# Softmax attention by head pairs on row and column groups of TensorE, in a fused two-layer block

## The chip, the cores and the metric

The kernel runs on one core of a Trainium2 chip. The metric is the device time of one execution in microseconds; the lower the better. All data are fp32.

## What is computed

Two layers over 1024 tokens of 1024 features. The first has four attention branches of four heads of 64 each; the second mixes a convolution, one more attention (E) and two short filters, and ends with a feed-forward part. The change concerns the softmax attention only, of which there are four kinds. Cut to what matters:

```python
# B: banded, window 128, with a sink (called SWA in the kernel)
# A, part 1: compressed keys (32 of them); part 2: selected blocks, here all of them (SEL)
# A, part 3: banded, window 512 (WIN)
s = einsum("qhd,khd->hqk", q, k) * Dh**-0.5 - slope[h] * (q_pos - k_pos)
p = masked_softmax(s, mask, sink)            # rows of queries, over keys
o = einsum("hqk,khd->qhd", p, v)
y_a = g0 * o_cmp + g1 * o_sel + g2 * o_win   # gates per token and head
# E: forgetting attention (FGT), c = cumsum(log_sigmoid(f))
s = q @ k * Dh**-0.5 + c[q] - c[k];  o = softmax(s, causal) @ v
```

SWA, SEL, WIN and FGT have 4 heads and 8 blocks of 128 queries each. A block of queries sees at most 2, 8, 5 and 8 blocks of keys. Everything else in the layers is projections: products of 1024 x 1024 activations with blocks of 128 weight columns.

## The kernel before

Each engine has its own program, written by walking one list of events, `TIMELINE`. The list is made by hand-written rules: the dense work is cut into parts, ("dense", block, part), one part being one 128-deep slice of a block, six matmuls of 512 columns (three products, since an fp32 operand is split into a high and a low fp32r part). The function `spread` lays the steps of an attention stage between the dense parts in proportion to a weight that `weight(ev)` gives each step. Each engine executes its share of each event in this order, so an engine that waits at one event holds back all its later ones, the dense parts too.

One softmax step before is ("soft", u): `unit(u)` is one head `h` and one block `i` of queries, 128 units in all, 32 to each of SWA, SEL, WIN and FGT. The step is a software pipeline over three units:

- PE (`soft` on the tensor engine): the value products of unit u-3 (L865: weights are the transposed probabilities in `ptr`, which is `pbuf[1]`, 128 x 128; 64 value columns stream), the transposes of unit u-2 in groups of four blocks (L843, into `ps6`), then the scores of unit u (L894: 64 rows, since a head is 64 deep; three products of up to 512 key columns, into `ps4`), and masks by bf16 matmuls (L897, L899). The trace counts a fp32 value product as two records, an fp32r product and a transpose as one.
- DVE: adds the bias to the scores (L1893, L1889) into one of three ring buffers `sring`, takes the negated maximum (L1899), makes the factor, 1 over the sum times the gate, in small steps (L1872 to L1879), and scales the output of unit u-3 into `ytok`, tokens on partitions (L1854, L1859).
- ACT: the exponential with its sum (L1318), the copies of the transposes from `ps6` to `ptr` (L1309), the high part of the next query tile (L1384); POOL makes its low part (L1598). Both heads of a pair use one query tile, 128 features.

The softmax output in `ytok` is turned to features on partitions by `ytrans` (L738, eight transposes for each half of a branch) before it is multiplied with the gate `z`. FGT needs the row of c over all keys on every partition; four broadcasts (L1052) make it, one for each head, and ACT copies it to `cb` (L1377). In the second layer, DVE copies the two transposed halves of E out (L2183) in the event "mix".

SWA lies between the parts of merge block D, SEL and WIN between those of merge block C (80 parts each), behind the five steps of the compressed branch (`cmp`, with pauses), and FGT between projections of layer 2, with DVE's convolution taps also in the list.

Of the kernel before, what the change touches and what calls it, by code (L numbers as in the profile page):

```python
# [7 lines left out]
ALU = mybir.AluOpType  # L8
# [89 lines left out]
def weight(ev):  # L98

    if ev[0] == "soft":  # L100
        u, first, n = ev[1:]
        return 1.5 + sum(0.5 * unit(v)[4] for v in (u, u - 2) if first <= v < first + n)
    if ev[0] == "stick" and ev[1] < NSTICK:
        return 1.0 + (HALF - stick_q0(ev[1])) / P
    return 5.0 if ev[0] == "pause" else 2.0
# [19 lines left out]
def unit(u):  # L125

    ph, r = ("SWA", "SEL", "WIN", "FGT")[u // 32], u % 32
    if ph == "FGT":
        h, i = r // NB, r % NB
    else:  # L130
        h, i = 2 * (r // 16) + r % 2, r % 16 // 2
    lo = {"SWA": max(0, i - 1), "SEL": 0, "WIN": max(0, i - 4), "FGT": 0}[ph]
    return ph, h, i, lo, i + 1 - lo

KTILE = [{"SWA": unit(u)[1] // 2, "SEL": 0, "WIN": 1, "FGT": unit(u)[1] // 2}[unit(u)[0]] for u in range(128)]
KSPLITS = [u for u in range(128) if u == 0 or (unit(u)[0], KTILE[u]) != (unit(u - 1)[0], KTILE[u - 1])]

QKEY = [(unit(u)[0], unit(u)[1] // 2, unit(u)[2]) for u in range(128)]  # L140
QFIRST = [u for u in range(128) if u == 0 or QKEY[u] != QKEY[u - 1]]
QLAST = [u - 1 for u in QFIRST[1:]] + [127]
QID = [int(np.searchsorted(QFIRST, u, side="right")) - 1 for u in range(128)]


def batches(u):
    return -(-unit(u)[4] // 4)

FAC_STEPS = [2 if unit(u)[0] == "FGT" else 3 for u in range(128)]
FAC_END = [int(v) for v in np.cumsum(FAC_STEPS)]
BATCH_END = [int(v) for v in np.cumsum([batches(u) for u in range(128)])]


NRET, NSTICK, NSWA, NSEL, NWIN, NFGT = NB, H * 12, 32, 32, 32, 32
U_SWA, U_SEL, U_WIN, U_FGT = 0, 32, 64, 96
# [14 lines left out]
def soft_events(first, n):  # L172
    out = []
    for u in range(first, first + n + 3):
        if u < first + n and u in KSPLITS:
            out.append(("ksplit", u))
        out.append(("soft", u, first, n))
    return out
# [51 lines left out]
def list_timeline():  # L230
# [3 lines left out]
    def z_events(br):  # L234
        ev = dense_part_events([br + "z0", br + "z1"])
        return ev + [("ytrans", br, 0), ("ytrans", br, 1)]
# [56 lines left out]
def number_tiles():  # L293

    g, tiles = 0, {}
    for ev in TIMELINE:
# [10 lines left out]
        elif ev[0] == "mix":  # L307
            tiles["yE0"] = g
            g += 2
# [2058 lines left out]
```

## Time and profile before

| | |
|---|---|
| median of 3 runs | 2836.91 us (2834.41 to 2838.14) |
| profiled execution | 2837.19 us, span 2835.2 us |
| PE busy | 2659.4 us, 94% of the span |
| PE weight loads | 2120.9 us, 75% |
| DVE, ACT, POOL busy | 918.7, 818.8, 876.7 us (32%, 29%, 31%) |
| mean granted clock of PE | 0.956 |
| DMA | 134.84 MB moved, queues 13.4% busy at most |
| value products, L865 | 936 records, 124.9 us busy |
| scores, L894 | 528 records, 182.9 us busy |
| transposes of probabilities, L843 | 468 records, 87.0 us busy |

[...] What a matmul costs in a stream is the distance from its start to the next start, and that is read from the timeline. Where the same line appears in two rows of a group view (different buffers), the table adds them.

### The profile page before, as it was taken

How to read it: one execution, taken by the hardware profiler on the slowest of the kernel's cores; microseconds unless marked ns; L12 is line 12 of the kernel's file. 1: busy time of each engine (PE TensorE's matmuls, PEld its weight loads, DVE VectorE, ACT ScalarE, POOL GpSimd, SP SyncE). 2: the span in 40 equal slices, each digit the busy share in tenths (PEclk: the TensorE clock that was granted, in tenths of full speed). 3: DMA queues.
4: the chain of work that ended last, by engine and by line, in shares of the span. 5: the costliest groups of instructions: out<-in, count | busy, mean ns of one | idle time of the engine just before them, and what ended most of it. 6: DMA issues, size and time to landing. Idle time of an engine off the chain costs nothing.

```text
span 2835.2 us, 30314 instructions
## 1 busy us (share of the span) xinstructions
PE 2659.4 (94%) x12580; PEld 2120.9 (75%) x12580; DVE 918.7 (32%) x1435; ACT 818.8 (29%) x1219; POOL 876.7 (31%) x492
## 2 busy tenths in 40 slices
PE   7798999999997998999999899898999999999896
PEld 5677778666686777787777677687888888888785
DVE  5213430323203544411237557404022222222423
ACT  4103441344322444422232333223211111111321
POOL 2122112444322111134642121235333323333633
PEclk8899999999998999999989899999999999999898
DMA  7001101100011000011212000120111111111111
GB/s 292 31 29 37 38 25 48 34 19 19 15 52 53 10 19 12 14 47 43 100 41 98 23 23 15 39 101 23 52 52 45 45 52 45 52 52 45 51 38 69
DMA packets 34440, 134.84 MB, mean 48 GB/s; under 512 B 3648, under 2 KB 4096, under 8 KB 32896
## 3 DMA queue, kind: packets, MB, share of 16 engines
q1 hardware_dynamic: 33984, 131.85, 13.4%
q8 instruction: 101, 1.65, 0.2%
q10 hardware_dynamic: 320, 1.05, 0.1%
q14 instruction: 35, 0.29, 0.0%
HBM read 123.45 MB, written 8.39 MB: 47 GB/s over the span
## 4 chain that ended last, share of the span: by engine, by line
PE 88%; DVE 5%; ACT 3%; POOL 2%; issue 1%; DMA 0%; POOLq 0%; SPq 0%; ACTq 0%; DVEq 0%
PE slot L667 55%; PE slot L713 12%; PE ps L894 4%; PE ps L865 3%; PE ps L843 2%; PE ps L745 2%; PE ps L927 1%; PE ps L918 1%; PE ps L931 1%; PE ps L944 1%; DVE cacc L2103 1%; PE ps L788 1%; POOL wlo L1505 1%; PE ps L771 1%; ACT zs L1233 0%
## 5 line engine op out<-in xcount | busy, mean ns | idle before, releaser
L667 PE MATMUL slot<-xhi,whi 128*128 128x512 f32 x2192 | 715.2, 408 | 59.2 <-ACT zs L1233 16.8
L667 PE MATMUL slot<-xlo,whi 128*128 128x512 f32 x2192 | 691.9, 397 | 0.0
L667 PE MATMUL slot<-xhi,wlo 128*128 128x512 f32 x2192 | 687.7, 395 | 0.0
L1505 POOL TENSOR_TENSOR wlo<-raw,whi 128x1024 fp32r<-128x1024 f32 (+1 forms) x169 | 429.6, 2542 | 832.3 <-ACT whi L1141 832.3
L667 PEld LDWEIGHTS slot<-xhi,whi 128*128 128x128 f32 x2192 | 404.9, 193 | 147.9 <-issue 66.1
L667 PEld LDWEIGHTS slot<-xlo,whi 128*128 128x128 f32 x2192 | 421.6, 192 | 92.1
L667 PEld LDWEIGHTS slot<-xhi,wlo 128*128 128x128 f32 x2192 | 420.0, 192 | 92.1
L1141 ACT ACTIVATE whi<-raw 128x1024 fp32r<-128x1024 f32 (+1 forms) x169 | 186.1, 1101 | 332.9 <-PE slot L713 174.1
L713 PE MATMUL slot<-uhi,whi 128*128 128x512 f32 x512 | 158.3, 390 | 0.0
L713 PE MATMUL slot<-ulo,whi 128*128 128x512 f32 x512 | 157.7, 389 | 0.0
L713 PE MATMUL slot<-uhi,wlo 128*128 128x512 f32 x512 | 157.6, 389 | 0.0
L1576 POOL TENSOR_TENSOR ulo<-tbuf,uhi 128x1024 fp32r<-128x1024 f32 x32 | 77.7, 2430 | 220.8 <-ACT uhi L1280 220.8
L865 PEld LDWEIGHTS ps<-brv,pbuf 128*128 128x128 f32 x936 | 129.4, 199 | 20.0 <-ACT cb L1377 5.8
L1776 DVE TENSOR_TENSOR mm<-slot,mm 128x1024 f32<-128x1024 f32 x56 | 68.6, 1225 | 229.2 <-PE slot L713 228.3
L1764 DVE SCALAR_TENSOR_TENSOR tbuf<-slot,tab 128x1024 f32<-128x1024 f32 x32 | 39.2, 1224 | 302.4 <-PE slot L667 302.3
L1309 ACT ACTIVATE pbuf<-ps 128x512 f32<-128x512 f32 (+3 forms) x176 | 79.7, 453 | 181.9 <-PE ps L843 180.3
L865 PE MATMUL ps<-brv,pbuf 128*128 128x64 f32 x936 | 124.9, 277 | 5.7 <-ACT cb L1377 3.3
L1562 POOL TENSOR_TENSOR mm<-mm,zs 128x1024 f32<-128x1024 f32 x24 | 58.1, 2423 | 210.2 <-DVE zs L1715 210.2
L1280 ACT ACTIVATE uhi<-tbuf 128x1024 fp32r<-128x1024 f32 x32 | 33.9, 1060 | 297.0 <-DVE tbuf L1767 297.0
L713 PEld LDWEIGHTS slot<-uhi,whi 128*128 128x128 f32 x512 | 95.5, 188 | 22.4 <-issue 3.0
L713 PEld LDWEIGHTS slot<-ulo,whi 128*128 128x128 f32 x512 | 96.1, 188 | 20.1
L713 PEld LDWEIGHTS slot<-uhi,wlo 128*128 128x128 f32 x512 | 96.1, 188 | 20.1
(326 smaller groups left out, 3054.0 us busy)
## 6 DMA issues: line engine op xcount, KB each, us to landing
raw<-wstream SPq DMA_DIRECT2D x129, 512.0 KB, 3.2
raw<-wstream SPq DMA_DIRECT2D x40, 640.0 KB, 3.9
ada<-wada SPq DMA_DIRECT2D x7, 1024.0 KB, 19.9
mm<-xT SPq DMA_DIRECT2D x2, 2048.0 KB, 9.8
ada<-wada SPq DMA_DIRECT2D x2, 2048.0 KB, 27.1
mm<-xT SPq DMA_DIRECT2D x8, 512.0 KB, 4.5
res_dram<-mm SPq DMA_DIRECT2D x8, 512.0 KB, 3.0
res<-res_dram SPq DMA_DIRECT2D x8, 512.0 KB, 6.5
```

The lines of the kernel that those rows point to most:

```text
L667: o = mm_(outs[:, half * HALF:(half + 1) * HALF], w[b % 2][:, k_w, :], x[:, k_x, half * HALF:(half + 1) * HALF], start=first and j == 0, s ...
L713: o = mm_(slot[(g + t) % 2][:, half * HALF:(half + 1) * HALF], w[:, kc, t, :], x[:, kc, half * HALF:(half + 1) * HALF], start=kc == 0 and ...
L745: o = mm_(ps7[:, place * NB + tb:place * NB + tb + 1], src[:, tb * P:(tb + 1) * P], t_("ones", 0, 1), start=first and tb == 0, stop=last a ...
L843: o = nc.tensor.transpose(ps6[:, (c - 4 * bi) * P:(c - 4 * bi + 1) * P], sring[m % 3][:, c * P:(c + 1) * P], t_("ident"))
L865: o = mm_(ps7[:, 0:DH], ptr[:, c * P:(c + 1) * P], v, start=c == 0, stop=c == nb - 1)
L894: o = mm_(ps4[:, c0:c1], q_[r0:r0 + DH, :], k_[r0:r0 + DH, lo * P + c0:lo * P + c1], start=j == 0, stop=j == 2)
L1141: nc.scalar.activation(flat(whi[b % 2])[:, 0:n], (raw1 if b == 1 else raw)[:, 0:n], ACT.Copy).then_inc(w_hi, 1)
L1309: nc.scalar.activation(ptr[:, bi * HALF:bi * HALF + w], ps6[:, 0:w], ACT.Copy).then_inc(s_ptsb, 1)
L1505: tt(flat(wlo[b % 2])[:, 0:n], (raw1 if b == 1 else raw)[:, 0:n], flat(whi[b % 2])[:, 0:n].bitcast(F32), ALU.subtract).then_inc(w_lo, 1)
L1562: tt(mm[:, n, :], mm[:, n, :], zs[0][:], ALU.add).then_inc(sum_done, 1)
L1576: tt(ulo[:, n, :], tbuf[n % 2][:], uhi[:, n, :].bitcast(F32), ALU.subtract).then_inc(u_lo, 1)
L1776: v.tensor_tensor(mm[:, n, :], slot[gg % 2][:], mm[:, n, :], ALU.add).then_inc(slot_free[gg % 2], 1)
```

## The change

The unit becomes a pair: `pair(p)` is two neighbouring heads (t = 0 or 1) and one block of queries, 64 pairs, 16 to a stage. Outside SWA, the blocks come in the order 0, 7, 1, 6, 2, 5, 3, 4 (`QORDER`). A pair's keys are cut into pieces of up to four blocks (one or two pieces, 88 in all). Per step:

- `scores(p, c)`: the same three products, but for both heads in turn, head a on array rows 64a to 64a+63, each into a PSUM bank of its own, `psb[a]`. The next piece waits until DVE has read both banks.
- `turn_p(p, a, c)`: the transposes of one head and one piece, still through the one bank `ps6`.
- `factor_rows(p)`: new. The factors of both heads (`fac`, one value per query) are laid out over 64 partitions each, behind the transposes of both heads, by one matmul per head with the identity; ACT copies this to `frow`.
- `values(p, c)`: operands are swapped. The value tile (128 x 64) is the weight, the transposed probabilities (128 columns) stream, and head a writes partitions 64a to 64a+63 of `ps7`, so the two heads are on the two column groups. The result has features on partitions, and DVE multiplies it with `frow` into `yfm` (`outputs`).
- `ytrans` is gone for B, A and E (six of ten transposes by eight); DVE multiplies `yfm` with `zs` directly ("ymul"), and "mix" splits `yfm` without the two copies.
- Queries are split one pair at a time, three pairs ahead ("qsplit"); there are twice as few of the other small steps, and the two reductions of a pair are one instruction.
- The compressed branch writes features on partitions too, and its gate is multiplied into the probabilities; its steps weigh 1.0 and its pauses 2.5 (before 2.0 and 5.0), while a softmax stage has lighter weights, set by explicit ("gap", w) events. So, of the parts of merge block C, five instead of two lie between the compressed scores (L976) and their transposes (L985), four instead of two between its last step and the first scores of SEL, and SEL begins after part 22 of 80 instead of part 12.
- FGT's row is made for both heads of a pair at once (two broadcasts for t = 0, two for t = 1, in `cb` and in the table `dist`), with one dense part between the two.

The places in the order of instructions. PE in the stage of SEL, before; `ps<-brv,pbuf` are value products, `ps<-tab,sbuf` and `ps<-tab,pbuf` transposes, `ps<-khi,qp` and `ps<-brkl,qp` scores, `slot<-` one dense part:

```order
L865 MATMUL ps<-brv,pbuf_76 128x64 x4
L843 MATMUL ps<-tab,pbuf_75 128x128 x4
L894 MATMUL ps<-khi,qp 128x512
L894 MATMUL ps<-brkl,qp 128x512
L894 MATMUL ps<-khi,qp 128x512
L894 MATMUL ps<-khi,qp 128x256
L894 MATMUL ps<-brkl,qp 128x256
L894 MATMUL ps<-khi,qp 128x256
L843 MATMUL ps<-tab,pbuf_75 128x128
L667 MATMUL slot<-yhi,whi_58 128x512 x2
L667 MATMUL slot<-ylo,whi_58 128x512 x2
L667 MATMUL slot<-yhi,wlo_60 128x512 x2
```

The same engine and stage with the change, for a pair of five key blocks; `ps<-tab,ring` are its transposes, `ps<-tab,fac` the factor rows, `ps<-ptr,brv` the values:

```order
L913 MATMUL ps<-tab,ring_81 128x128 x4
L923 MATMUL ps<-tab,fac 64x128 x2
L706 MATMUL slot<-xhi,whi_58 128x512 x2
L706 MATMUL slot<-xlo,whi_58 128x512 x2
L706 MATMUL slot<-xhi,wlo_60 128x512 x2
L937 MATMUL ps<-ptr,brv 64x128 x8
L913 MATMUL ps<-tab,ring_81 128x128
L898 MATMUL ps<-khi,qp 128x512 x2
L898 MATMUL ps<-brkl,qp 128x512 x2
L898 MATMUL ps<-khi,qp 128x512 x2
L913 MATMUL ps<-tab,ring_81 128x128
L937 MATMUL ps<-ptr,brv 64x128 x2
```

Each product now stands twice, once for each head. The values stood one unit behind their transposes, with other work between; now they stand one part or less behind them, and for the last piece here directly behind. The factor rows have a place of their own.

ACT in the same stage, before; `pbuf_76<-ps` is the copy of transposes, `den<-` an exponential, `zs<-slot` the sigmoid of a merge block, `whi<-raw` the split of a weight block:

```order
L1318 ACTIVATE pbuf_75,den<-pbuf_75,nmx 128x768
L1233 ACT_TABLE_LOAD
L1233 ACTIVATE zs_109<-slot 128x1024
L1141 ACTIVATE whi_58<-raw 128x1280
L1309 ACTIVATE pbuf_76<-ps 128x512
L1309 ACTIVATE pbuf_76<-ps 128x256
L1318 ACT_TABLE_LOAD
L1318 ACTIVATE sbuf_73,den<-sbuf_73,nmx 128x896
L1384 ACTIVATE qp<-brq 128x128
```

and with the change, where `ptr<-ps` is the copy of transposes and `frow<-ps` that of the factor rows:

```order
L1360 ACTIVATE ptr<-ps 128x384 x2
L1431 ACTIVATE frow<-ps 128x128
L1352 ACTIVATE ring_81,den<-ring_81,nmx 128x640 x2
L1275 ACT_TABLE_LOAD
L1275 ACTIVATE zs_113<-slot 128x1024
L1183 ACTIVATE whi_58<-raw 128x1280
L1426 ACTIVATE qp<-brq 128x128
L1360 ACTIVATE ptr<-ps 128x512 x2
L1431 ACTIVATE frow<-ps 128x128
L1352 ACT_TABLE_LOAD
L1352 ACTIVATE ring_80,den<-ring_80,nmx 128x512 x2
```

Two exponentials now follow one another, and behind them, with the sigmoid and the split of a merge block between, stand the copies that PE's next transposes and values wait for.

The core of the diff:

```diff
+def pair(p):
+    ph, r = ("SWA", "SEL", "WIN", "FGT")[p // 16], p % 16
+    t, i = r // 8, r % 8 if ph == "SWA" else QORDER[r % 8]
...
 def soft_events(first, n):
...
+    for p in range(first, last + 1):
+        score, bias = scored(p + 2, 0)
+        out += split(p + 2, p + 3) + [("turn_p", p, 0, 0)] + score + [("turn_p", p, 1, 0), ("frow", p)]
+        out += ([("exp", p + 1)] if p < last else []) + bias
+        if pieces(p) > 1:
+            score, bias = scored(p + 2, 1)
+            out += [("gap", 1.0), ("values", p, 0), ("turn_p", p, 0, 1), ("gap", 0.5)] + score
+            out += [("turn_p", p, 1, 1)] + bias + [("gap", 0.5), ("values", p, 1)]
+        else:
+            out += [("gap", 1.5), ("values", p, 0)]
...
+            def scores(p, c):
...
+                for j, (q_, k_) in enumerate(((q_h, k_h), (q_h, k_l), (q_l, k_h))):
+                    for a in range(2):
+                        r = slice(a * DH, a * DH + DH)
+                        o = mm_(psb[a][:, 0:w], q_[r, :], k_[r, c0:c0 + w], start=j == 0, stop=j == 2)
...
+            def factor_rows(p):
+                pe.wait_ge(s_fac, p + 1)
+                pe.wait_ge(s_norm, p)
+                for a in range(2):
+                    at_ = 2 * (p % 2) + a
+                    o = mm_(ps7[a * DH:a * DH + DH, P:2 * P], fac[:, at_:at_ + 1].to_broadcast([P, DH]), t_("ident"),
+                            start=True, stop=True)
+                o.then_inc(s_row, 1)
...
+            def values(p, c):
+                pe.wait_ge(s_ptsb, turn_index(p, 1, c) + 1)
+                if c == 0:
+                    pe.wait_ge(s_rowsb, p + 1)
...
+                for j in range(n):
+                    for a in range(2):
+                        o = mm_(ps7[a * DH:a * DH + DH, 0:P], value_tile(p, a, b0 + j), ptr[:, a, j * P:(j + 1) * P],
+                                start=b0 + j == 0, stop=b0 + j == pair(p)[4] - 1)
...
+            def outputs(p):
...
+                    v.tensor_tensor(y, ps7[:, 0:P], frow[:], ALU.mult).then_inc(s_norm, 1)
...
-                        v.tensor_copy(pbuf[t][:], slot[g % 2][:]).then_inc(slot_free[g % 2], 1)
-                        wait_evacuated(dve, "yE%d" % t)
-                        v.tensor_copy(token[:, 0:1], token[:, 1:2]).then_inc(mix_src, 1)
-                    split_wide(3, 4, 2, pbuf[0][:])
+                    split_wide(3, 4, 2, yfm[:, 0, :])
```

## Rows read from the trace of the kernel before

**Rows 1.** page, part 4: the chain that ended last, shares of the span.

```profile
PE 88%; DVE 5%; ACT 3%; POOL 2%; issue 1%; DMA 0%; POOLq 0%; SPq 0%; ACTq 0%; DVEq 0%
```

**Rows 2.** windows: stretch, us; PE, PEld, DVE, ACT, POOL busy (count); granted clock; DMA share; GB/s.

```profile
252.00:421.00 169.00, 156.56 (x772) 124.85 (x770) 69.10 (x232) 78.28 (x179) 33.54 (x26) 0.96 0.09 30
...
912.00:1210.00 298.00, 277.21 (x1527) 221.27 (x1520) 147.20 (x400) 136.06 (x286) 53.38 (x47) 0.94 0.05 15
1556.00:1782.00 226.00, 207.69 (x1072) 165.02 (x1072) 133.35 (x228) 78.22 (x168) 45.33 (x45) 0.93 0.07 21
```

**Rows 3.** line L894: count, ns min/median/max, first and last start, forms.

```profile
L894 PE MATMUL ps<-brkl,qp x128: 268/280/625, 259.2 to 1199.3; 64*128 64x512 f32 x44, 64*128 64x256 f32 x40, 64*128 64x128 f32 x32, 64*128 64x384 f32 x12
...
L894 PE MATMUL ps<-brkl,qpf x48: 271/388/412, 1568.2 to 1763.3; 64*128 64x512 f32 x24, 64*128 64x128 f32 x8, 64*128 64x256 f32 x8, 64*128 64x384 f32 x8
```

**Rows 4.** timeline of PE, one unit of WIN: start, us, instruction, form, count.

```profile
1101.16 1.00 PE L865 MATMUL ps<-brv,pbuf 128*128 128x64 f32 x8
1102.00 0.61 PE L843 MATMUL ps<-tab,pbuf 128*128 128x128 f32 x4
1102.54 0.50 PE L894 MATMUL ps<-khi,qp 64*128 64x512 f32 x1
1102.88 0.39 PE L894 MATMUL ps<-brkl,qp 64*128 64x512 f32 x1
1103.11 0.39 PE L894 MATMUL ps<-khi,qp 64*128 64x512 f32 x1
...
1103.75 0.27 PE L894 MATMUL ps<-brkl,qp 64*128 64x128 f32 x1
1103.87 0.27 PE L894 MATMUL ps<-khi,qp 64*128 64x128 f32 x1
1104.07 0.73 PE L667 MATMUL slot<-xhi,whi 128*128 128x512 f32 x2
1104.63 0.63 PE L667 MATMUL slot<-xlo,whi 128*128 128x512 f32 x2
1105.10 0.62 PE L667 MATMUL slot<-xhi,wlo 128*128 128x512 f32 x2
```

**Rows 5.** timeline of PE in the retention stage.

```profile
156.50 0.72 PE L804 MATMUL ps<-dq,dk 64*128 64x128 f32 x8
...
157.15 0.45 PE L811 MATMUL ps<-dv,dt 128*64 128x64 f32 x8
...
157.53 0.43 PE L829 MATMUL ps<-dv,sbuf 128*128 128x64 f32 x2
```

**Rows 6.** timeline of PE, products of 256 columns.

```profile
1025.21 0.28 PE L894 MATMUL ps<-brkl,qp 64*128 64x256 f32 x1
...
1025.33 0.28 PE L894 MATMUL ps<-khi,qp 64*128 64x256 f32 x1
```

**Rows 7.** groups of PE by line: form, count, busy us, mean ns, idle before.

```profile
L738 PE MATMUL slot<-tab,ytok 128*128 128x128 f32 x80 | 10.6, 276 | 1.4 <-ACT zs L1223 1.0 <-DVE scy L1754 0.4
```

**Rows 8.** timeline: transposes, the copy of them on ACT, the next transposes.

```profile
1202.26 0.61 PE L843 MATMUL ps<-tab,sbuf 128*128 128x128 f32 x4
...
1202.97 0.60 ACT L1309 ACTIVATE pbuf<-ps 128x512 f32<-128x512 f32 x1 [0.58 <-PE ps L843]
...
1203.62 0.33 PE L843 MATMUL ps<-tab,sbuf 128*128 128x128 f32 x1 [0.75 <-ACT pbuf L1309]
```

**Rows 9.** groups of DVE by line and form: the bias of 512 columns.

```profile
L1893 DVE SCALAR_TENSOR_TENSOR sbuf<-tab,ps 128x512 f32<-128x512 f32 x5 | 3.4, 687 | 5.2 <-PE ps L894 5.2
```

**Rows 10.** line L894: what its engine waited for (us, times).

```profile
  POOL qp L1598: 11.5, 4
```

**Rows 11.** timeline of PE: transposes of the compressed branch, idle before them.

```profile
902.22 1.12 PE L985 MATMUL ps<-tab,sbuf 128*128 128x128 f32 x4 [6.87 <-DVE sbuf L2009]
```

**Rows 12.** timeline of PE: behind a forget row.

```profile
1612.40 0.77 PE L865 MATMUL ps<-brv,pbuf 128*128 128x64 f32 x5 [1.11 <-ACT cb L1377]
```

**Rows 13.** timeline of DVE: the first copy of the transposed forgetting output.

```profile
1826.45 1.21 DVE L2183 COPY pbuf<-slot 128x1024 f32<-128x1024 f32 x1
```

More of the change, by code:

```diff
@@ L98, in weight @@
 def weight(ev):
-    if ev[0] == "soft":
-        u, first, n = ev[1:]
-        return 1.5 + sum(0.5 * unit(v)[4] for v in (u, u - 2) if first <= v < first + n)
+    if ev[0] == "gap":
+        return ev[1]
+    if ev[0] in ("scores", "bias", "exp", "factor", "frow", "turn_p", "values", "qsplit", "ksplit"):
+        return 0.0
+    if ev[0] == "cmp":
+        return 1.0
     if ev[0] == "stick" and ev[1] < NSTICK:
         return 1.0 + (HALF - stick_q0(ev[1])) / P
-    return 5.0 if ev[0] == "pause" else 2.0
+    return {"pause": 2.5, "row": 0.7, "fprep": 1.0}.get(ev[0], 2.0)
 NTAPS_EARLY = 28
@@ L172, in soft_events, with split, scored @@
 def soft_events(first, n):
[L173 to L177, printed above, removed]
+    last = first + n - 1
+    def split(p, q):
+        return ([("ksplit", p)] if p <= last and p in KSPLITS else []) + ([("qsplit", q)] if q <= last else [])
+    def scored(p, c):
+        if p > last or c >= pieces(p):
+            return [], []
+        rows = [("row", p, a) for a in range(2)] if c == 0 and pair(p)[0] == "FGT" and pair(p)[2] == 0 else []
+        return rows + [("scores", p, c)], [("bias", p, c)]
+    out = split(first, first) + split(last + 1, first + 1)
+    for p in (first, first + 1):
+        for c in range(pieces(p)):
+            out += sum(scored(p, c), []) + [("gap", 0.5)]
+        out += split(first + 1, last + 1) + [("exp", first)] if p == first else []
+    out += [("factor", first)] + split(last + 1, first + 2)
+    for p in range(first, last + 1):
[8 more added lines that the diff above has]
+            out += [("gap", 1.5), ("values", p, 0)]
+            for c in range(1, pieces(p + 2) if p + 2 <= last else 1):
+                out += sum(scored(p + 2, c), [])
+        if p < last:
+            out.append(("factor", p + 1))
+        if pieces(p) == 1:
+            out.append(("gap", 1.5))
     return out
@@ L235, in z_events @@
         ev = dense_part_events([br + "z0", br + "z1"])
-        return ev + [("ytrans", br, 0), ("ytrans", br, 1)]
+        return ev + [("ymul" if br in "BA" else "ytrans", br, n) for n in range(2)]
     tl = [("norm1",)]
@@ new lines, in forget_row @@
+            def forget_row(p, a):
+                t = pair(p)[1]
+                if (t, a) == (0, 0):
+                    pe.wait_ge(f_ci, 1)
+                    wait_evacuated(pe, "Ef")
+                pe.wait_ge(s_biased, 2 * PIECE0[p])
+                pe.wait_ge(f_cb, 2 * t + a)
+                h = 2 * t + a
+                for half in range(2):
+                    o = mm_(psb[half], t_("ident")[0:4, h:h + 1].to_broadcast([4, P]),
+                            ct[0:4, half * HALF:(half + 1) * HALF], start=True, stop=True)
+                o.then_inc(f_bc, 1)
@@ L1114, in _ @@
                 elif ev[0] == "mix":
[L1116 to L1118 removed]
+                    pe.wait_ge(s_norm, NPAIR)
                     pe.wait_ge(m_pw_in, 2)
```

473 lines of the change are left out of this document (221 added, 252 removed).

## Prediction

> **What bounds the kernel now.** I read the chain that ended last first: 88% of the span is PE's [rows 1]. So time goes down only where PE issues less or waits less. Then the stretches: in SWA, in SEL with WIN, and in FGT PE is busy 157 of 169, 277 of 298 and 208 of 226 us, while ACT and DVE are busy at most 60% [rows 2]. In these stages too it is the amount of PE's work that counts, with 12, 21 and 18 us of idle time, the starts of the stages included. Last the timeline of one unit [rows 4], read as distances from start to start, which gives prices at the higher clock level (2.4 GHz):
>
> - a value product record 0.105 us (eight in 0.84), though it streams only 64 columns; the next rows, transposes, cost 0.11 (four in 0.44, with 0.10 left over);
> - a score product of 512 columns 0.23, of 128 columns 0.12 (at row 1103.75 to 1103.87), of 256 columns 0.12 [rows 6]; 384 columns I put between, 0.18;
> - a dense part 1.4 us (0.47 for two of its six matmuls);
> - **a change of the array's shape**: the first 64-row product comes 0.10 late and the second starts 0.34 behind it, where the next distance is 0.23, so 0.10 more; back to 128 rows it is 0.20 instead of 0.12, and 0.56 instead of 0.47 for the first two dense matmuls. A visit to another shape costs 0.10 + 0.10 + 0.09 + 0.09 = 0.38.
>
> **Do two groups overlap?** This decides everything. In the retention stage heads alternate on row groups: eight records (four pairs) of 128 columns start in 0.65 us, 0.115 a pair once 0.19 of entering is taken off; next to them eight records on alternating column groups take 0.38, 0.07 a pair with the 0.10 of entering off [rows 5]. One alone would cost 0.115 for its 128 columns. So a pair costs what one costs. The score case (512 columns, two PSUM banks) differs from the row only in length. For the column groups the row has 64 streamed columns, the change 128; I take 0.115 a pair (the stream) and keep 0.23 (no overlap) as the other end.
>
> The Trainium skill ("TensorEngine Tiling (Array Packing)", Key Properties) says that changing the tiling mode drains the engine; by that rule, the trace agrees with 0.1 us on each side. It speaks against this change: the sum below has more visits.
>
> **The change part by part**, PE first.
>
> 1. *Scores.* Pieces per head are 68 of 512, 20 of 384, 48 of 256 and 40 of 128 columns (both of [rows 3] added); three products each: 3 x (68 x 0.23 + 20 x 0.18 + 48 x 0.12 + 40 x 0.12) = 89 us. Half of it goes: **-45** (none if row groups did not overlap).
> 2. *Values.* 936 records at 0.105 = 98 us become 468 pairs at 0.115 = 54: **-44**.
> 3. *Factor rows.* New, 64 pairs of heads, two records each head: 128 x 0.115 = **+15**.
> 4. *Visits.* Before, 128 units, and 16 of WIN with a mask between two pieces: 144 x 0.38 = 55. With the change 88 pieces of scores, 88 of values, 64 factor rows, 240 visits. For column groups the second entry costs less, since the weights are 64 columns: I take 0.34. 88 x 0.38 + 152 x 0.34 = 85: **+30**.
> 5. *Output transposes.* 48 of the 80 of L738 go [rows 7], at 0.11: **-5**. The multiply that followed them is DVE's before and after, and its result is wanted eight dense parts (11 us) later: nothing more. Six fewer small waits for a slot: within the rounding.
> 6. *Transposes, masks*: the same number, nothing.
>
> These six make -49. What moves between waits:
>
> 7. *Compressed branch.* PE stands 6.9 us before the transposes L985, behind a chain on DVE [rows 11]. Three more parts (4.2 us) now stand there, and two more ahead of SEL's first scores, where the wait is POOL's query split, four times in all [rows 10]: **-6**. DVE has one small operation more in that chain. SWA's start waits for the key split as before: 0.
> 8. *Forget rows.* Behind each of four broadcasts PE waits about 1.1 us for the copy [rows 12]; two of the four now have a dense part in the gap: **-2**. FGT's first wait (for DVE's backlog of taps) stays.
> 9. *Mix.* DVE's two copies of 1.2 us go from its queue [rows 13], ahead of the product PE waits for; 1.7 of the 2.5 is in item 5: **-1**.
> 10. *New waits.* Before, a copy of transposes had a whole unit's time. When nothing stood between, at the drain of WIN, the next transposes started 1.36 us behind the first ones, that is 0.9 of waiting: 0.27 until ACT starts, 0.60 of copy, the rest semaphores [rows 8]. With the change both heads go through the same bank, with only scores between, and the values follow half a "gap" later, which in SEL and WIN is often no part at all (58 parts for 32 pairs). Going down the new order with 0.9 as the latency behind four transposes, and less for fewer, I find 38 places with too little work in between, 26 us in all, 15 of them values directly behind their transposes. On top, ACT's sigmoid, its table load and the weight split stand in that queue once per merge block (six in these stages), about 2 us each; and DVE, with two biases of up to 0.69 [rows 9] and a joint reduction ahead of the factor, can be late for the factor row behind a pair of eight key blocks. These overlap with one another, so I take half of 24: 12. Together 38; less about 16 of waits that go (POOL's query splits, ACT's copies, a third of the 51 us of idle time of [rows 2]): **+22**. Bounds: 0 if the cover holds everywhere, +45 if nothing overlaps.
>
> Sum: -49 - 6 - 2 - 1 + 22 = **-36**. Against the profiled execution's own 2837.2 us (its span of 2835.2 and 2.0 around it) that is 2801; this execution lies 0.3 above the median, so 2801 stands for the median too. The clock I leave as it is: 0.96, 0.94 and 0.93 in the three stages [rows 2], so some 35 us are already paid there for the lower level.
>
> DVE, ACT and POOL are not the bound on the average: the same elements pass; DVE loses many instructions of 0.15 us; POOL's splits are as many and now three pairs ahead, so PE should not meet them.
>
> **The rivals.**
>
> - *The cover holds*: waits no larger than before. For it: all engines but PE are under 60% busy [rows 2], and queries, biases and exponentials stand a full pair ahead. Against it: the ends in item 10. Time: 2801 - 22 = 2779. Chance 0.2.
> - *The chain through ACT is the new bound of a pair*: exponentials of two heads stand ahead of the second piece's copies, and each of the 48 pairs outside SWA waits 0.8 us longer than I took. Time: 2801 + 38 = 2839, no change. For it: a cover of under two parts per pair. Chance 0.08; with half of it (2820) another 0.14, inside my range.
> - *Packing pays less.* The Trainium skill ("TensorE: Matmul & The Clock Gate", Measured speedup vs the span model) gives 3.07 times for four row tiles and not four. As a mechanism here: the 0.65 us of the four pairs on row groups [rows 5] holds no price of entering, and a pair costs 0.16 instead of 0.115. With 264 pairs of score products, 468 of values and 128 of factor rows that is 860 x 0.045 = 39 more: 2840. Against it: the column groups beside it take 0.38 for as many. Chance 0.04.
> - *Slower: column groups do not overlap when each streams 128 columns of its own.* Then values cost 936 x 0.115 = 108 instead of 54, and factor rows 30 instead of 15: 69 more, 2870. The point from which it decides: a pair of value records at over 0.18 us. Against it: eight such records with 64 columns took 0.38 [rows 5]. Chance 0.04.
> - *The clock falls for longer*, since short products, transposes and 96 more shape changes take the place of dense streams in SEL and WIN. For it: 0.94 and 0.93 there already. To eat 38 us, PE would need 76 us more at the lower level (1.2 GHz), of some 640 in these stages, twice as much as now; half of that gives 2820. Chance 0.06 for the whole, 2839 or more.
>
> **The numbers.** My forecast with its neighbourhood (2787 to 2817) has 0.44. The range reaches from the case of the held cover with a little more from the clock, 2770, to the half cases at 2820 and some way beyond them, 2828; beyond it are about 0.2. A measurement tells 0.2%, 6 us, from no change. Faster by more than that (under 2831): 0.87; within it 0.06 (the ACT chain in full, packing at 1.3); slower 0.07 (column groups, clock).
>
> **What the profile of the changed kernel would show.** Items 1 and 2: score records of the two heads starting within 0.01 us of each other and a piece of 512 columns in about 0.9 us; eight value records in about 0.5 us. Item 4: first records in a shape 0.1 late on 240 visits. Item 10: PE idle before transposes and values, released by the copies on ACT, 25 to 40 us in all; an idle of over 60 would make the ACT rival true. Item 7: idle before the compressed transposes of about 3 us. The three stages together should shrink from 693 us to about 660, less what the compressed branch took of their parts; the first scores of SEL come later. I am wrong if pairs of records do not start together, if the granted clock of these stages falls under 0.88, or if DVE turns out to hold PE.

## The result, and the profile after

The changed kernel takes **2808.6 us** in the median (2807.6 to 2810.2, four runs) beside 2837.5 us for the kernel before on the same chip: a ratio of 0.9898 (95% interval 0.9886 to 0.9910), 29 us faster. The forecast was 2801, so the direction held and 7 us of the gain are missing. The profiled execution took 2809.5 us, its span is 2807.4, its mean granted clock 0.952 (before: 0.956). One execution of e10 below lasted 9043 us at a granted clock of 0.27; its numbers are those of the other three.

The page of the changed kernel, part 1:

```profile
PE 2608.7 (93%) x12788; PEld 2027.6 (72%) x12788; DVE 893.2 (32%) x1192; ACT 818.1 (29%) x1265; POOL 871.2 (31%) x476
```

PE is busy 50.7 us less, but the span is only 27.8 us shorter: PE now stands idle 2807.4 - 2608.7 = 198.7 us where it stood 175.8. The windows of the three stages, in the columns of [rows 2]:

```profile
252.00:416.00 164.00, 153.09 (x845) 113.80 (x846) 50.75 (x138) 80.48 (x194) 33.81 (x25) 0.97 0.10 31
905.00:1196.00 291.00, 247.78 (x1706) 170.06 (x1704) 140.06 (x304) 136.28 (x318) 51.84 (x46) 0.93 0.05 16
1556.00:1752.00 196.00, 179.19 (x1086) 127.29 (x1085) 120.56 (x171) 71.37 (x160) 33.30 (x26) 0.94 0.06 20
```

SWA and FGT stand idle as much as before (11 and 17 us). SEL with WIN lost 29 us of busy time and gained 22 of idle time, 43 instead of 21. The window of the changed kernel begins ahead of SEL and holds about two dense parts fewer; taken from block start to block start (869.2 to 1209.4 and 864.6 to 1196.4), 28 us of busy time went and 20 of idle time came, 51.4 instead of 31.4. The groups of PE by line show whom it waits for (last column: idle before, and what ended it):

```profile
L706 PE MATMUL slot<-xhi,whi 128*128 128x512 f32 x2192 | 718.6, 410 | 50.8 <-DVE xlo L2226 15.3 <-ACT zs L1275 11.0 <-DVE xlo L1890 6.4
...
L913 PE MATMUL ps<-tab,ring 128*128 128x128 f32 x468 | 86.7, 288 | 9.1 <-ACT ptr L1360 8.8
L937 PE MATMUL ps<-ptr,brv 128*64 128x128 f32 x936 | 72.6, 288 | 11.1 <-ACT ptr L1360 8.5 <-ACT frow L1431 2.5
...
L898 PE MATMUL ps<-khi,qp 64*128 64x512 f32 (+3 forms) x256 | 48.3, 385 | 21.4 <-POOL qp L1646 13.8 <-issue 5.2 <-DVE ring L1910 2.5
...
L923 PE MATMUL ps<-tab,fac 128*64 128x128 f32 x256 | 30.4, 319 | 22.7 <-DVE fac L1938 16.6 <-DVE fac L1934 6.0
```

The factor rows L923 alone wait 22.7 us for the factor of VectorE, as much as all of the growth (other waits came and went too, see the items below). Copies on ACT hold the transposes and values only 8.8 + 8.5 + 2.5 = 20 us. The timeline of one pair, with DVE beside PE (rows of weight loads are left out):

```profile
996.71 1.09 PE L937 MATMUL ps<-ptr,brv 128*64 128x128 f32 x16
997.74 0.33 PE L913 MATMUL ps<-tab,ring 128*128 128x128 f32 x1
998.00 0.50 PE L898 MATMUL ps<-khi,qp 64*128 64x512 f32 x2
998.33 0.40 PE L898 MATMUL ps<-brkl,qp 64*128 64x512 f32 x2
998.57 0.39 PE L898 MATMUL ps<-khi,qp 64*128 64x512 f32 x2
998.89 0.33 PE L913 MATMUL ps<-tab,ring 128*128 128x128 f32 x1
...
1000.65 2.29 DVE L1917 TENSOR_REDUCE nmx<-ring 128x2 f32<-128x2048 f32 x1
...
1002.85 0.28 DVE L1950 TENSOR_TENSOR frow<-ps,frow 128x128 f32<-128x128 f32 x1
1003.16 0.29 DVE L1951 TENSOR_TENSOR yfm<-frow,yfm 128x128 f32<-128x128 f32 x1
...
1003.77 0.16 DVE L1938 TENSOR_TENSOR fac<-fac,gates 128x2 f32<-128x2 f32 x1
...
1003.99 0.69 PE L923 MATMUL ps<-tab,fac 128*64 128x128 f32 x4 [2.45 <-DVE fac L1938]
```

The overlap is there: sixteen value records take 1.03 us (997.74 less 996.71) where eight took 0.84 [rows 4], and a piece of 512 columns for both heads 0.89. But DVE works through the joint maximum (2.29 us), the output and only then the factor, and PE waits 2.45 us.

The span splits into three terms, counted over PE's records: idle time; what the lower clock level costs (half of the busy time in stretches granted 1.2 GHz); and the rest, the work as it would be at 2.4 GHz.

| kernel | span | idle | lower level | work |
|---|---|---|---|---|
| before | 2835.2 | 175.8 | 86.5 | 2572.9 |
| changed | 2807.4 | 198.7 | 90.8 | 2518.0 |
| e7, both heads on the same rows | 2864.3 | 187.3 | 119.7 | 2557.3 |
| e5, queries split late | 2852.7 | 230.1 | 107.6 | 2515.0 |
| e8, maximum behind the factor | 2795.1 | 191.3 | 86.7 | 2517.1 |
| e4, factor rows behind the values | 2770.4 | 192.3 | 78.0 | 2500.2 |
| e12, e4 with two moves more | 2765.7 | 187.8 | 79.5 | 2498.5 |

The change saves 55 us of work, gives back 23 in waits and 4 in clock (the last is no more than that term differs between two kernels of equal work, see the end). By the starts of the merge and projection blocks, the stretch of SWA went from 172.3 to 167.0 us, that of the compressed branch with SEL and WIN from 340.2 to 331.8, that of FGT from 225.2 to 210.3: 29 us together, the whole gain (forecast: 33).

### The profile page after: what moved, and what is told of

It is laid out like the page before. It is cut to its first block, busy times and chain, and to the rows that moved or that the text cites. A ratio compares the mean times of both kernels' runs of the same rounds, so it can differ in the third digit from the quotient of the medians.

```text
span 2807.4 us, 30549 instructions
## 1 busy us (share of the span) xinstructions
PE 2608.7 (93%) x12788; PEld 2027.6 (72%) x12788; DVE 893.2 (32%) x1192; ACT 818.1 (29%) x1265; POOL 871.2 (31%) x476
## 4 chain that ended last, share of the span: by engine, by line
PE 87%; DVE 6%; issue 3%; ACT 3%; POOL 1%; DMA 0%; POOLq 0%; SPq 0%; ACTq 0%; DVEq 0%
PE slot L706 57%; PE slot L752 12%; PE ps L913 2%; PE ps L937 2%; PE ps L898 2%; PE ps L784 2%; PE ps L976 1%; PE ps L967 1%; PE ps L980 1%; PE ps L993 1%; DVE cacc L2159 1%; PE ps L923 1%; PE ps L827 1%; PE ps L810 1%; POOL wlo L1554 1%
## 5 line engine op out<-in xcount | busy, mean ns | idle before, releaser
L1360 ACT ACTIVATE ptr<-ps 128x256 f32<-128x256 f32 (+3 forms) x176 | 79.9, 454 | 276.3 <-PE ps L913 275.9
L1910 DVE SCALAR_TENSOR_TENSOR ring<-tab,ps 128x256 f32<-128x256 f32 (+3 forms) x128 | 57.2, 488 | 136.3 <-PE ps L913 125.4
L913 PE MATMUL ps<-tab,ring 128*128 128x128 f32 x468 | 86.7, 288 | 9.1 <-ACT ptr L1360 8.8
```

The lines of the kernel that those rows point to most:

```text
L913: o = nc.tensor.transpose(ps6[:, j * P:(j + 1) * P], ring[p % 2][:, a, (b0 + j) * P:(b0 + j + 1) * P], t_("ident"))
L1360: nc.scalar.activation(ptr[:, a, 0:w], ps6[:, 0:w], ACT.Copy).then_inc(s_ptsb, 1)
L1910: ins = v.scalar_tensor_tensor(out=dst, in0=t_("dist", o, w), scalar=SLOPES[2 * t + a], in1=psb[a][:, 0:w], op0=ALU.mult, op1=ALU.add)
```

## The experiments

Ratios are to the kernel before, timed on the same chip; the changed kernel has 0.9898. Differences in us are between medians of different chips, on which the kernel before took 2836.9 to 2839.0; the ratios are the firmer comparison.

**e1: the factor earlier on VectorE.**

```diff
+            early = [("factor", p + 1)] if p < last else []
...
-            out += [("turn_p", p, 1, 1)] + bias + [("gap", 0.5), ("values", p, 1)]
+            out += [("turn_p", p, 1, 1)] + early + bias + [("gap", 0.5), ("values", p, 1)]
...
-        if p < last:
-            out.append(("factor", p + 1))
```

(for pairs of one piece it goes ahead of the values)

> Edit: on VectorE each pair's factor is worked out ahead of the next scores' last bias and joint maximum instead of behind them; TensorE's order is untouched. Theory (the gain was lost because the factor rows of TensorE wait for VectorE's factor, 36.6 + 13.3 us of idle before L923): the idle before the factor rows falls under 15 us and the kernel gets 15 to 35 us faster than the changed kernel, 2775 to 2795. Rival A (that wait only stands in front of another, the copies on ScalarE): the idle before L923 goes but comes back before transposes and values, time 2800 to 2812. Rival B (VectorE is simply late with everything, so the factor moves and the bias is late in its place): idle before the scores L898 behind the bias grows, time 2805 or more.

Measured: 2810.6 us, 0.9899 (0.9882 to 0.9916): nothing gained, rival A's time, but by none of the three mechanisms: idle before the transposes and values stays (8.8 and 11.1 us, in the changed kernel 9.1 and 11.1), and that before the scores of the first layer grows by 1 us. The group of the factor rows in e1:

```profile
L922 PE MATMUL ps<-tab,fac 128*64 128x128 f32 x256 | 30.5, 318 | 18.5 <-DVE yfm L1950 11.0 <-DVE yfm L1952 3.8 <-DVE fac L1937 1.9
```

The releaser has changed its name: the rows also wait until the output of the pair before has been read out of their bank, and that output stands behind the same joint maximum. In the first trace this second wait was hidden, since a wait for two semaphores is put down to the later one.

**e2: values of the two heads apart.**

```diff
-                for j in range(n):
-                    for a in range(2):
+                for a in range(2):
+                    for j in range(n):
```

> Edit: the value products of the first head all stand before those of the second, so that no two neighbours lie on different column groups; same products, same shapes. If two column groups overlap (a pair costs what one costs): 468 pairs lose their overlap, 468 x 0.105 to 0.115 us = 49 to 54 us more, 2855 to 2863. If column groups do not overlap at 128 streamed columns: no change, 2808. Small waits may hide a little of it: 2845 at the least.

Measured: 2826.5 us, 0.9960 (0.9949 to 0.9972), 18 us slower than the changed kernel: a miss, between the two cases. The timeline of e2, a piece of sixteen records:

```profile
1102.00 1.55 PE L937 MATMUL ps<-ptr,brv 128*64 128x128 f32 x16 [0.64 <-ACT frow L1431]
1103.49 0.33 PE L913 MATMUL ps<-tab,ring 128*128 128x128 f32 x1
```

1.49 us instead of 1.03, while pieces of eight records (four of one head, then four of the other) took the same 0.39 from first to last start in both kernels, in pairs 7 and 13 ns apart. From the starts, sixteen records take 1.31 instead of 0.82 and twelve 0.87 instead of 0.60: the second head starts beside the first head's fifth of eight, and third of six. So PE starts a record on a free column group about four records ahead of its turn, and only what is farther away loses its partner: 34 pieces of four blocks x 0.49 + 10 of three x 0.27 = 19 us, the 18 that were measured. (The profile does not name the head of a record; that two records are of different heads is read from starts 6 ns apart, where those of one head lie 109 apart.) The overlap is real; the edit took away a good third of it.

**e3: scores of the two heads apart** (the same exchange of the two loops in `scores`).

> Edit: the three score products of one head stand before the three of the other, so that the two row groups are hardly ever busy together; same products. If row groups overlap fully: 45 us more (half of the 89 us of score products), less the part at the change of head where they still overlap (one product in three, about 15 us): 2835 to 2855. If they do not overlap: no change, 2808.

Measured: 2811.3 us, 0.9904 (0.9886 to 0.9923), no change. The timeline of e3 says why:

```profile
997.91 0.50 PE L898 MATMUL ps<-khi,qp 64*128 64x512 f32 x2
...
998.25 0.40 PE L898 MATMUL ps<-brkl,qp 64*128 64x512 f32 x2
998.48 0.40 PE L898 MATMUL ps<-khi,qp 64*128 64x512 f32 x2
```

The program issues three products of one head, then three of the other, and the records still start in pairs 10 ns apart. The experiment did not test what it was made for.

**e7: both heads' scores on the same rows.** The second head's scores are not computed; the first head's stand in their place.

```diff
-                        r = slice(a * DH, a * DH + DH)
+                        r = slice(0, DH)
```

> Edit: the score products of both heads are taken from the first head's 64 rows (so the second head's scores are not computed; the first head's stand in their place). Shapes, order and waits stay, but no two neighbours lie on different row groups. e3 showed that putting one head's three products first does not part them: the records of the two heads still started 10 ns apart. If the overlap of row groups is what paid for the scores, this gives back half of the 89 us of score products: 2808 + 35 to 48 = 2843 to 2856. If the gain at the scores came from something else (fewer changes of shape, fewer waits): under 2820.

Measured: 2862.7 us, 1.0085 (1.0065 to 1.0106), 54 us slower than the changed kernel, a little above the range. By the table, whose profiled execution is 3.5 us longer than the median, 39 us are work, against the 45 of item 1, and 29 are the lower clock level, less 11 of waits that longer scores cover. The overlap of row groups alone carries more than the whole gain.

**e5: queries split directly ahead of their scores.**

```diff
-    out += [("factor", first)] + split(last + 1, first + 2)
+    out += [("factor", first)]
...
-        out += split(p + 2, p + 3) + [("turn_p", p, 0, 0)] + score + [("turn_p", p, 1, 0), ("frow", p)]
+        out += split(p + 2, p + 2) + [("turn_p", p, 0, 0)] + score + [("turn_p", p, 1, 0), ("frow", p)]
```

> Edit: each query is split directly ahead of its own pair's scores instead of one pair earlier, so that ScalarE's rounding and GpSimd's subtraction (0.30 + 0.45 us and two semaphores) stand before the scores. Theory (the prediction's: PE should not meet the splits where they are three pairs ahead, and waited for them four times before): some 60 places, of which those with GpSimd busy on a weight split or a merge sum wait 1 to 3 us: 10 to 30 us slower, 2818 to 2838. Rival (splitting early hides nothing that was not hidden): 2806 to 2811.

Measured: 2854.8 us, 1.0063 (1.0048 to 1.0078): 46 us slower than the changed kernel and slower than the kernel before. The sign was right, the size not. A group and a place in the timeline of e5:

```profile
L898 PE MATMUL ps<-khi,qp 64*128 64x512 f32 (+3 forms) x256 | 51.3, 404 | 61.8 <-POOL qp L1646 56.5 <-DVE ring L1910 2.6 <-DVE brkl L2133 2.6
```

```profile
1041.28 2.34 POOL L1611 TENSOR_TENSOR mm<-mm,zs 128x1024 f32<-128x1024 f32 x1 [12.61 <-DVE zs L1763]
1043.58 0.45 POOL L1646 TENSOR_TENSOR qp<-brq,qp 128x128 fp32r<-128x128 f32 x1
1044.14 0.32 PEld L898 LDWEIGHTS ps<-khi,qp 64*128 64x128 f32 x2 [4.01 <-issue]
1044.18 0.79 PE L898 MATMUL ps<-khi,qp 64*128 64x512 f32 x2 [3.80 <-POOL qp L1646]
```

The query waits behind the merge sum in POOL's queue. POOL is busy a third of the time, but its single instructions are 2.3 to 2.9 us long. Waits for the split grow from 13.8 to 56.5 us; idle time as a whole grows by 31 and the lower level costs 17 more (table).

**e8: only the joint maximum moved, behind output and factor.**

```diff
         if p < last:
             out.append(("factor", p + 1))
+        if p + 2 <= last:
+            out.append(("reduce", p + 2))
```

> Edit: only VectorE's order is changed: the joint maximum of two pairs ahead stands behind the output's multiply and the factor instead of ahead of both; TensorE's order is the changed kernel's. e1 moved the factor alone and gained nothing: the factor rows then waited 18.5 us for the output (VectorE yfm) in its place, which stands behind the same maximum. Theory (one queue, two things that the factor rows wait for, both behind the joint maximum of up to 2.29 us): the idle before the factor rows falls from 50 to under 20 us and the time to 2775 to 2792. Then what e4 has beyond this (2772.7) is the price of 64 visits less. Rival (all of e4's 36 us came from the visits): 2805 to 2811.

Measured: 2800.1 us, 0.9870 (0.9856 to 0.9885), 8.5 us faster than the changed kernel, between the theory's range and the rival's. The waits of the factor rows are more than halved:

```profile
L926 PE MATMUL ps<-tab,fac 128*64 128x128 f32 x256 | 29.6, 312 | 10.2 <-DVE fac L1944 8.4 <-DVE fac L1940 1.6
```

The theory's place is right, its size was wrong: I had summed idle time of matmuls and of weight loads (36.6 + 13.3), which count the same wait twice. There were 22.7 us to be had. And not all of them stand behind the maximum: two single waits, 3.38 and 3.66 us, have another cause, given in the last section, and e8 leaves 1.82 and 3.66 us at these places.

**e4: factor rows behind the values, in the shape the array has already.** The joint maximum goes behind the output here too, but ahead of the factor, and it is the values, not the factor rows, that wait for the output of the pair before.

```diff
-        out += split(p + 2, p + 3) + [("turn_p", p, 0, 0)] + score + [("turn_p", p, 1, 0), ("frow", p)]
+        out += split(p + 2, p + 3) + [("turn_p", p, 0, 0)] + score + [("turn_p", p, 1, 0)]
...
-            out += [("turn_p", p, 1, 1)] + bias + [("gap", 0.5), ("values", p, 1)]
+            out += [("turn_p", p, 1, 1)] + bias + [("gap", 0.5), ("values", p, 1), ("frow", p)]
...
+        if p + 2 <= last:
+            out.append(("reduce", p + 2))
...
                 if c == 0:
-                    pe.wait_ge(s_rowsb, p + 1)
+                    pe.wait_ge(s_norm, p)
```

> Edit: the factor rows stand directly behind the pair's last value products, which have the same shape, instead of between transposes and values; the joint maximum of two pairs ahead comes behind the output's multiply on VectorE, and the values wait for the output of the pair before. Theory: 64 visits of another shape go (64 x 0.34 = 22 us by the price of the prediction) and most of the 50 us of waiting for the factor goes, but values may now wait for ScalarE's copy and VectorE's multiply: 2750 to 2785. Rival (the copy of the factor row and the multiply are the new bound, since they must end before the next values start): idle before the values L937 grows by over 30 us and the time stays at 2800 to 2815. If a visit costs nothing when it is only a change of shape, the gain is that of the waits alone, 2775 to 2795.

Measured: 2772.7 us, 0.9772 (0.9754 to 0.9789), 36 us faster than the changed kernel. Groups of PE in e4:

```profile
L916 PE MATMUL ps<-tab,ring 128*128 128x128 f32 x468 | 87.6, 290 | 12.4 <-ACT ptr L1362 11.9
L939 PE MATMUL ps<-ptr,brv 128*64 128x128 f32 x936 | 71.8, 286 | 13.3 <-ACT ptr L1362 11.5 <-DVE yfm L1956 1.8
L925 PE MATMUL ps<-tab,fac 128*64 128x128 f32 x256 | 25.6, 279 | 2.1 <-DVE fac L1943 2.0
```

The factor rows wait 2 us, the values 2 us more, not 30. Beside e8 the work is 17 us less, for 64 visits: 0.26 us each, against the 0.34 of the prediction. The other term is the clock: 9 us less at the lower level than e8; all four executions of e4 were granted 0.956 to 0.958, those of e8 0.952 to 0.954. Why is not shown. Waits in all are the same as in e8: what the factor rows no longer wait stands before the slots of the dense work, whose waits for ACT's sigmoid grow from 11.4 to 17.9 us, and before transposes and values, 3 and 2 us more.

**e9: e4 with the second query of a stage behind its first scores.**

> Edit: e4, and at the start of each of the three stages the second query is split behind the first scores instead of ahead of them. TensorE waits 13.8 us for the query splits at the starts. Theory: the second split on GpSimd (0.45 us, 0.94 beside VectorE's key split) goes from two or three such waits: 1 to 3 us faster than e4, 2769 to 2772. Rival: the wait is for what stands ahead of both splits; no change, 2772.7.

Measured: 2774.9 us, 0.9785 (0.9768 to 0.9801), no change, the rival. Waits for the splits at the starts are 13.8 us in both, 8.45 before SWA's first scores and 5.4 before SEL's: they wait for what stands ahead of both queries.

**e10 and e12: two moves on top of e4.** e10 puts ACT's copy of the factor row, with DVE's output and joint maximum behind it, half a gap later for pairs of one piece; its edit against e4:

```diff
+        out += ([("gap", 0.75)] if pieces(p) == 1 else []) + [("fcopy", p)]
...
-            out.append(("gap", 1.5))
+            out.append(("gap", 0.75))
```

e12 also moves a half gap; its edit against e10:

```diff
-            out += [("gap", 1.0), ("values", p, 0), ("turn_p", p, 0, 1), ("gap", 0.5)] + score
-            out += [("turn_p", p, 1, 1)] + bias + [("gap", 0.5), ("values", p, 1), ("frow", p)]
+            out += [("gap", 1.0), ("values", p, 0), ("turn_p", p, 0, 1)] + score
+            out += [("turn_p", p, 1, 1)] + bias + [("gap", 1.0), ("values", p, 1), ("frow", p)]
```

> Edit: e4, and for pairs of one piece ScalarE's copy of the factor row (and VectorE's multiply and joint maximum behind it) stand half a gap later than TensorE's factor rows. In e4 ScalarE stood 1.8 us before that copy with the merge sigmoid behind it, so TensorE waited 1.22 us for a slot in most blocks of SWA, and SWA took 169.7 us against 167.0 of the changed kernel. Theory (the copy blocks the sigmoid): those waits go, SWA falls to 162 to 165 us and the kernel to 2764 to 2769. Rival (the sigmoid's table load is what is late, as in every block): no change, 2772.7; or the later multiply holds the next pair's values: over 2775.

> Edit: e10, and for pairs of two pieces the half gap between the second piece's transposes of the first head and the next scores is moved behind the transposes of the second head, ahead of the values. The scores (0.9 us) cover the first copy by themselves; the dense part covers the second. Theory: of the 12 + 13 us that TensorE waits for ScalarE's copies in e4 some 5 to 8 go: 4 to 8 us faster than e10. Rival (scores alone do not cover the first copy, since exponentials of 2 x 1.3 us stand ahead of it on ScalarE): the waits before transposes grow, as many us slower.

Measured: e10 2767.3 us, 0.9750 (0.9732 to 0.9767); SWA, from its first merge matmul to the next block, takes 163.6 us instead of 169.7, as expected. e12 2765.1 us, 0.9736 (0.9715 to 0.9757), less than the 4 to 8 us that were expected; its interval overlaps that of e10, so the 2 us between them are not settled. The rows of e12:

```profile
L917 PE MATMUL ps<-tab,ring 128*128 128x128 f32 x468 | 86.5, 287 | 12.4 <-ACT ptr L1363 11.7
L940 PE MATMUL ps<-ptr,brv 128*64 128x128 f32 x936 | 71.4, 284 | 7.8 <-ACT ptr L1363 5.3 <-DVE yfm L1957 2.4
```

The values' wait for the copy fell from 11.5 us in e10 to 5.3, but other waits took its place: idle before transposes grew from 11.0 to 12.4, before factor rows from 2.1 to 4.0, before the scores of the first layer from 24.0 to 25.9, and idle time in all is 187.8 us beside 186.0. So the move gained no waiting. e12 is the fastest kernel measured: 74 us faster than the kernel before in the same comparison, 44 faster than the change.

**e11: the old weights of the compressed branch, with the changed kernel's softmax stages.**

```diff
-    if ev[0] == "cmp":
-        return 1.0
...
-    return {"pause": 2.5, "row": 0.7, "fprep": 1.0}.get(ev[0], 2.0)
+    return {"pause": 5.0, "row": 0.7, "fprep": 1.0}.get(ev[0], 2.0)
```

> Edit: of the change only the weights of the compressed branch and its pauses are undone (back to 2.0 and 5.0), all else is the changed kernel. The prediction gave the new weights 6 us (4.2 us of parts into a wait of 6.9 before the compressed transposes, and two parts ahead of SEL's first scores). Theory of the prediction: 3 to 8 us slower, 2812 to 2817. Rival, from the changed kernel's trace: the wait only moved to the slot behind ScalarE's late sigmoid (5.05 us), so the new weights won nothing, and the old ones leave fewer dense parts for the pairs: 2806 to 2812, or 2812 to 2820 by the pairs' lost cover, in which case the waits before transposes and factor rows grow and not that of the compressed branch.

Measured: 2810.2 us, 0.9899 (0.9884 to 0.9914), no change, inside the rival's range. But the edit does not bring the old places back. The dense parts are laid out in proportion to the weights, and those of the softmax stages stayed light: six parts now lie between the compressed scores and their transposes (before two, changed five), and SEL's first scores come behind part 34 of block C (before 12, changed 22). The timeline of the changed kernel at that place:

```profile
895.81 1.05 PE L706 MATMUL slot<-yhi,wlo 128*128 128x512 f32 x2
...
898.38 1.06 ACT L1461 ACTIVATE sbuf<-sbuf 128x1024 f32<-128x1024 f32 x1 [12.83 <-DVE sbuf L2048]
...
900.75 1.02 ACT L1275 ACTIVATE zs<-slot 128x1024 f32<-128x1024 f32 x1
...
901.92 1.19 PE L706 MATMUL slot<-xhi,whi 128*128 128x512 f32 x2 [5.05 <-ACT zs L1275]
```

and of e11:

```profile
906.42 1.06 ACT L1459 ACTIVATE sbuf<-sbuf 128x1024 f32<-128x1024 f32 x1 [12.61 <-DVE sbuf L2046]
...
909.96 0.70 PE L704 MATMUL slot<-xhi,whi 128*128 128x512 f32 x2 [0.85 <-ACT zs L1273]
...
912.16 0.66 PE L1032 MATMUL ps<-tab,sbuf 128*128 128x128 f32 x4 [0.57 <-DVE sbuf L2057]
```

In the changed kernel ACT waits 12.8 us for DVE before the branch's exponentials, and the merge sigmoid that must empty PE's slot stands behind them. The block of columns that fills this slot ends one part behind the compressed scores, so the dense parts that were to fill the old wait of 6.9 us [rows 11] cannot be issued: the wait has moved 8 us ahead. In e11 it ends five parts behind them, and both waits are under 1 us. From the start of the compressed branch up to SEL's first scores PE stands idle 13.9 us in the kernel before, 14.2 in the changed one and 7.9 in e11; from there to the end of merge block C, that is in the pairs of SEL and WIN, 17.5, 37.2 and 42.2. So e11 won 6 us at the branch and paid 5 for them in the pairs, which have fewer parts as cover. What the changed kernel would take with the old places was not run.

## Why the prediction was right, and where it was off

**Do two groups overlap?** Right, for both kinds. A pair of value records costs 0.109 us (taken: 0.115), a pair of score products what one cost. The rival on packing (0.16 a pair) falls with this price, and the slower one, no overlap of column groups, with it and with e2. The Trainium skill ("TensorEngine Tiling (Array Packing)", Key Properties) also says that different tiles can execute in parallel; the traces agree, and show more, that neighbours in the program need not be on different tiles (e2, e3).

**Items 1 to 6**, forecast at -49, came out at -55 of work. Item 1: -39 by e7, not -45 (e7 takes away the overlap alone). Item 2: 98 to 468 x 0.109 = 51, so -47, not -44. Item 3: 128 x 0.11 = +14. Item 4: the price of a visit with column groups is 0.26 (e4 against e8, factor rows alone), not 0.34; if it holds for the values too, 152 visits cost 12 us less, +18 instead of +30. With item 5 that makes -59; 4 of it I cannot place.

**Item 7** failed: -6 forecast, nothing came, 13.9 us of idle time before and 14.2 after. The 6.9 us before the transposes are gone, but 5.05 stand before a slot, and SEL's first scores wait 5.4 us for POOL's query split in place of 3.3, in spite of two parts more ahead of them. The step that failed is the one that put parts into the wait and did not ask whether ACT, in its own order, would still empty the slots; e11 shows that the wait does go when the block of columns ends later behind the scores, at the price of the pairs' cover.

**Items 8 and 9.** Item 8 was right: the value products of FGT waited 3.3 us for the copy of the row (L1377) before and wait for it nowhere now. FGT's first wait, for DVE's key split, which I left unchanged, shrank from 8.5 to 2.3 us; the cause is open. The mix became no faster: PE waits 10.9 us there where it waited 9.0.

**Item 10** is the term that was mis-sized. Items 7 to 10 together were forecast as +13 of waiting; idle time grew by 23. Less the parts above (+0.3, -3.3, +1.9 and FGT's -6.2) that leaves +30 for item 10, forecast at +22. I gave half of 24 us to "the sigmoid, the table load and DVE late for the factor row", as if one cause hid the other. The factor rows alone wait 22.7. I had listed the two biases and the joint maximum as "behind a pair of eight key blocks", but not costed the maximum: it runs over both heads, 2048 elements in 2.29 us, and both things the factor rows wait for stand behind it (e1, e8) in most places; 7.0 of the 22.7 us have another cause (last section). The copies on ACT, for which I had 26 us, hold PE 20, so the ACT rival is far off. Of the 16 us of waits that were to go, those for POOL's query splits did not: 12.9 before, 13.8 after. The rival that the cover holds is out with all this. And one of my own signs of being wrong came true: "if DVE turns out to hold PE". It does, in the factor rows.

**The clock**, left as it was, costs 4 us more: the rival's sign, not its size, and not clear of that term's own spread.

**The total** is nearer than its parts. Work came out 6 us better than forecast, waits 10 worse and the clock 4 worse; that the sum is only 7 off is in part luck. What the prediction had right is the mechanism that pays, the overlap; of the waits it had the sum too small and the main holder wrong.

## What to carry to other kernels

When a step waits for several semaphores, moving the producer that the profile names only brings the next name forward: look up every wait in the code and ask what all of them stand behind. A small operation in a queue costs what the longest instruction ahead of it lasts, so on engines that are idle most of the time put long reductions behind, and splits a whole pair ahead of, what TensorE waits for. With the array in column groups, put work of the same shape side by side before looking for more overlap.

## What the hardware showed that was not expected

**Records start ahead of their turn.** On a free column group PE starts a matmul some four records early (e2), and on a free row group at least three, which hides an order of three and three entirely (e3). The depth is read from pieces of two lengths, not tried with other patterns.

**Small VectorE operations last as long as a GpSimd one beside them.** In the changed kernel, around one pair:

```profile
1106.84 2.37 POOL L1611 TENSOR_TENSOR mm<-mm,zs 128x1024 f32<-128x1024 f32 x1 [8.19 <-DVE zs L1763]
1106.99 2.37 DVE L1951 TENSOR_TENSOR yfm<-frow,yfm 128x128 f32<-128x128 f32 x1
...
1109.17 2.93 POOL L1554 TENSOR_TENSOR wlo<-raw,whi 128x1280 fp32r<-128x1280 f32 x1
1109.29 2.84 DVE L1931 TENSOR_SCALAR den<-den 128x2 f32<-128x2 f32 x1
...
1112.58 0.48 PE L923 MATMUL ps<-tab,fac 128*64 128x128 f32 x2 [3.38 <-DVE fac L1938]
...
1151.38 2.34 POOL L1611 TENSOR_TENSOR mm<-mm,zs 128x1024 f32<-128x1024 f32 x1 [11.04 <-DVE zs L1763]
1151.53 2.33 DVE L1951 TENSOR_TENSOR yfm<-frow,yfm 128x128 f32<-128x128 f32 x1
...
1154.65 0.69 PE L923 MATMUL ps<-tab,fac 128*64 128x128 f32 x4 [3.66 <-DVE fac L1938]
```

L1951 takes 0.29 us elsewhere and L1931 0.16, for two elements a partition; here each ends within 0.2 us of POOL's instruction, and PE waits 3.38 and 3.66 us, with no joint maximum ahead of the factor. These two waits are 7.0 of the 22.7 us of item 10. Three of the 32 of L1951 and three of the 64 of L1931 are stretched so, 13 us in all. Not every meeting stretches: L1950, which reads one of its inputs from PSUM, lies beside such an instruction of POOL five times and takes at most 0.29 us each time. The Trainium skill ("SBUF — State Buffer", SBUF: two separate sides) has GpSimd share a pair of ports with those VectorE instructions that have two SBUF inputs or run in a two-port mode, and one instruction holds the pair to its end; by that rule, the trace agrees. A version that keeps GpSimd out of the way was not tried.

**The lower clock level does not follow the waits.** In e5, 31 us more of waiting came with 17 more for the lower level; but e7, with 11 us less of waiting and longer scores, has 29 more, and e10, with 6 us less of waiting than e4, has 7 more (84.7 and 78.0). What decides is not shown. Between e1 and the changed kernel, whose idle time and work differ by less than 1 us each, the term differs by 4, so differences of that size mean nothing.
